# Ten expert weight blocks loaded ahead of the routed experts in place of eight, and the first four experts written out ahead of the loop

## The chip, the cores and the metric

One Trainium2 chip, one core. The metric is the device time of one launch in microseconds (us); the kernel before takes 1544.34 us, the median of three runs from 1542.98 to 1544.42.

## What is computed

Two transformer blocks over 256 tokens of width 1024, all in f32. The first block is a token mixer (sliding window attention beside a gated spatial unit), a layer norm, a layer of 32 routed experts (each token goes to 4) and a second layer norm. The second block (a recurrent mixer beside a block attention, then a convolutional FFN) follows; the change does not touch it.

```python
def expert_block(args):                       # per expert e, its tokens xb
    gt = jnp.minimum(xb @ w_gate[e] + b_gate[e], SWIGLU_LIMIT)
    up = jnp.clip(xb @ w_up[e] + b_up[e], -SWIGLU_LIMIT, SWIGLU_LIMIT)
    hid = gt * jax.nn.sigmoid(SWIGLU_ALPHA * gt) * (up + 1.0)
    return hid @ w_down[e] + b_down[e]
# first block: x = LN1(ALPHA1*x + mixer(x));  x = LN2(ALPHA1*x + sum over 4 experts of gate*expert(x))
```

Each expert has three 1024x1024 f32 matrices, 12 MB; all 32 are read once, 403 MB.

## The kernel before

**Blocks and slots.** The host lays an expert's weights out as 6 blocks of 2 MB, 4096 floats in each of 128 partitions: 4 "up" blocks (gate and up matrices) and 2 "down" blocks. There are 192 blocks, numbered here as loads 0 to 191 in the order of use. They go through a ring of `RING` = 8 slots in SBUF: slots 0 to 5 are the tensor `ring`, slots 6 and 7 are pieces of the tensor `work`. Load n lies in slot n % 8.

**Who waits for whom.** TensorE (PE) counts the semaphore `slots_used` up by one after the matmuls of each block (L746 for up, L776 for down). SyncE (SP) issues all weight loads on one queue, in program order. Load n from 8 on is issued in `refill` once `slots_used` is at least n - 7, so when the block that lies 8 before it has been used:

```python
sp.wait_ge(slots_used, sp.snap(it * (TURN * SLOTS) + (load - RING + 1)))
sp.dma_start(slot_area(s), expert_slot(e, load % SLOTS)).then_inc(slot_in[s], 16)
```

PE waits for `slot_in[s]` before a block's first matmul (L738, L769).

**The stage before the experts.** SP first issues the token mixer's inputs and weights. The last two are `x` (L470) and five broadcast rows of 1024 floats (`rows`, L471: `b_out`, `ln1_g`, `ln1_b`, `ln2_g`, `ln2_b`). VectorE (DVE) waits for these two before L1608. SP then waits for the end of attention (`attn_done`) to issue the expert biases (L474), and then loads 0 to 7 as the mixer's weights, whose room the slots share, fall free: 0, 1, 2, 3 and 6 after the projections, 4 and 5 behind two steps of the output projection, 7 last (L476 to L493), behind five small loads for the second block.

**The experts.** PE, ScalarE (ACT), DVE and SP each run a loop over 8 iterations of `TURN` = 4 experts (L778, L1305, L1753, L505), with counts from the router's result. In an expert PE does 4 up blocks (L743), gathers the next expert's tokens (L695), transposes, does 2 down blocks (L774) and scatters the result (L707) in the next one.

**Behind the experts.** SP issues the first weight halves of the second block into ring slots 0 and 1: `lora` (two halves of 0.75 MB) and `r` (L521), once `slots_used` says that slots 0 to 3 are free. GpSimd (POOL) casts the first lora half (L2118), DVE subtracts (L1770, called by `rest_half("lora", (0,))` at L1772), and only then does DVE, in its program order, start the second layer norm (L1630, from L1776). ACT casts the second lora half (L1314), then loads its table and does the norm's square root (L1329).

Of the kernel before, what the change touches and what calls it, by code (L numbers as in the profile page):

```python
# [16 lines left out]
P = 128  # L17
T = 256
TT = T // P
D = 1024  # L20
KD = D // P
# [8 lines left out]
PASSES = T // CAP  # L30
COLS = NE * PASSES + 2
# [4 lines left out]
RING = 8  # L36
TURN = 4
PER_TURN = TURN * SLOTS // RING
SPLITS = 3
# [76 lines left out]
def program(nc, A, out):  # L116
    ctx = ExitStack()
    with ctx:
# [11 lines left out]
        work, work_parts = area("work", 27500)  # L130
# [3 lines left out]
        def take(floats):  # L134
            a = work[:, top[0]:top[0] + floats]
            top[0] += floats
            assert top[0] <= 27500, top
            return a
# [36 lines left out]
        n_iter = ctx.enter_context(nc.sbuf_tensor("n_iter", [1, 2], I32))  # L175

# [27 lines left out]
        chosen4 = sq.rearrange("p t c -> p (t c)")[:, 0:TT * TOPK * NE].rearrange("p (t k e) -> p t k e", t=TT, k=TOPK)  # L204
# [4 lines left out]
        hid, yy = pool2[:, 0:512], pool2[:, 512:1024]  # L209
        hidT = pool2[:, 1024:1536].rearrange("p (j c) -> p j c", j=4)  # L210
# [10 lines left out]
        consts_in, w_g_in, w_u_in = sem("consts_in"), sem("w_g_in"), sem("w_u_in")  # L221
        ln_rows_in, wsT_in = sem("ln_rows_in"), sem("wsT_in")
# [217 lines left out]
        def slot_of(turn, j):  # L440

            return (turn * SLOTS + j) % RING

        def landed_count(it, turn, j):

            return (it * PER_TURN + (turn * SLOTS + j) // RING + 1) * 16

        def up_slot(s):

            return slot_area(s).rearrange("p (b k n) -> p b k n", b=2, k=2)  # L450

        def down_slot(s):
            return slot_area(s).rearrange("p (k n) -> p k n", k=4)

        @block.sync
        def _(sp):
# [8 lines left out]
            sp.dma_start(w_in[:, :, W_QKV + G1:], A["w_in"][:, :, W_QKV + G1:]).then_inc(w_g_in, 16)  # L465
# [4 lines left out]
            sp.dma_start(x_nat, A["x"].rearrange("(t p) d -> p t d", p=P)).then_inc(ln_rows_in, 16)  # L470
            sp.dma_start(rows_sb[:, 0:mix_at], A["rows"][0:mix_at].partition_broadcast(P)).then_inc(ln_rows_in, 16)  # L471
# [4 lines left out]
            for s in (0, 1, 2, 3, 6, 4, 5, 7):  # L476
# [5 lines left out]
                if s == 5:  # L482
                    sp.wait_ge(mix_done, 4)
# [9 lines left out]
                sp.dma_start(slot_area(s), expert_slot(s // SLOTS, s % SLOTS)).then_inc(slot_in[s], 16)  # L493
# [4 lines left out]
            def refill(it, load):  # L498

                s = load % RING  # L500
# [56 lines left out]
        def _(pe):  # L557
# [41 lines left out]
            pe.wait_ge(w_g_in, 16)  # L599
# [128 lines left out]
            def expert(it, turn):  # L728

                now, ahead = pe.snap(it * TURN + (turn + 1)), pe.snap(it * TURN + (turn + 2))  # L730
# [5 lines left out]
                for j in range(UP_SLOTS):  # L736
                    s = slot_of(turn, j)
                    pe.wait_ge(slot_in[s], pe.snap(landed_count(it, turn, j)))  # L738
                    w = up_slot(s)
                    for kk in range(2):  # L740
                        for b, to in enumerate((gate_bank, up_bank)):
                            for n2 in range(2):
                                ins = pe.matmul(to[n2 * CAP:(n2 + 1) * CAP, :], x_e[:, 2 * j + kk, :],  # L743
                                                w[:, b, kk, n2 * BANK:(n2 + 1) * BANK],
                                                start=False, stop=j == UP_SLOTS - 1 and kk == 1)
# [21 lines left out]
                for j in range(SLOTS - UP_SLOTS):  # L767
                    s = slot_of(turn, UP_SLOTS + j)
                    pe.wait_ge(slot_in[s], pe.snap(landed_count(it, turn, UP_SLOTS + j)))  # L769
                    w = down_slot(s)  # L770
                    for kk in range(4):
                        k = 4 * j + kk
                        for n2 in range(2):
                            ins = pe.matmul(y_bank[n2 * CAP:(n2 + 1) * CAP, :], hidT[:, k % 4, k // 4 * CAP:(k // 4 + 1) * CAP],  # L774
                                            w[:, kk, n2 * BANK:(n2 + 1) * BANK], start=False, stop=k == KD - 1)
                    ins.then_inc(slots_used, 1)  # L776

            with pe.Fori(0, n) as it:  # L778
# [438 lines left out]
        def _(act):  # L1217
# [75 lines left out]
            def expert(it, turn):  # L1293

                now, ahead = act.snap(it * TURN + (turn + 1)), act.snap(it * TURN + (turn + 2))
# [6 lines left out]
                act.wait_ge(slots_used, act.snap(it * (TURN * SLOTS) + (turn + 1) * SLOTS))  # L1302
                act.copy(yy, bank[7][:, :]).then_inc(y_ready, 1)  # L1303

            with act.Fori(0, n) as it:  # L1305
# [218 lines left out]
        def _(dve):  # L1524
# [82 lines left out]
            dve.wait_ge(ln_rows_in, 32)  # L1607
# [127 lines left out]
            def expert(it, turn):  # L1735

                now = dve.snap(it * TURN + (turn + 1))
                dve.wait_ge(slots_used, dve.snap(it * (TURN * SLOTS) + (turn * SLOTS + UP_SLOTS)))
# [14 lines left out]
            with dve.Fori(0, n) as it:  # L1753
# [19 lines left out]

            for t in range(TT):
# [428 lines left out]
```

## Time and profile before

| | |
|---|---|
| median of 3 runs | 1544.34 us |
| profiled execution | 1542.65 us, span 1540.5 us |
| granted TensorE clock, mean | 0.994 |
| PE / DVE / ACT / POOL busy | 93% / 33% / 21% / 4% of the span |
| stages | mixer to 117 us, experts 117 to 1031 us, second block to the end |
| chain of work that ended last | PE 58%, DMA 34%, DVE 5%, ACT 2% of the span |

The profiled execution takes 2.15 us more than its span. The chain of work is followed back from the last instruction, at each step to what released it. Times in the rows are from the start of the span.

### The profile page before, as it was taken

The page shows a single profiled execution, that of the slowest core. Times are in us where ns is not written, and L with a number is a line of the kernel's source. Part 1 is how long each engine was busy: PE and PEld are TensorE (multiplying, and loading weights), DVE is VectorE, ACT ScalarE, POOL GpSimd, SP SyncE. Part 2 cuts the span into 40 slices and gives each one's busy share as a digit, 9 for nine tenths or more (in the row PEclk, how much of TensorE's full clock was granted, in tenths as well). Part 3 has the DMA queues.
Part 4 walks back from the last instruction along what each step waited for, and adds up shares of the span by engine and source line. Part 5 has one row for each costly group of instructions (what it writes and reads, how often), then busy time and mean ns, then how long its engine had stood idle before and what let it go on. Part 6 is the DMA issues. An engine that isn't in the chain of part 4 may idle for free.

```text
span 1540.5 us, 21839 instructions
## 1 busy us (share of the span) xinstructions
PE 1437.0 (93%) x9246; PEld 783.7 (51%) x9246; DVE 512.3 (33%) x880; ACT 329.8 (21%) x480; POOL 64.8 (4%) x32
## 2 busy tenths in 40 slices
PE   8989999999989989989998998978999999999998
PEld 6543333333333333333333333328878895499997
DVE  1762211112112112112111111137797455365665
ACT  0531110001001001001000000015555220244442
POOL 0000000000000000000000000000000000022231
PEclk9999999999999999999999999998999999999999
DMA  9589999999999999999999999983441106145552
GB/s 363 225 343 403 428 427 428 429 428 429 429 429 428 428 429 429 429 428 429 428 429 428 428 429 429 428 355 110 164 164 55 56 2 246 41 157 198 177 191 82
DMA packets 44533, 491.33 MB, mean 319 GB/s; under 512 B 4944, under 2 KB 5456, under 8 KB 13168
## 3 DMA queue, kind: packets, MB, share of 16 engines
q1 hardware_dynamic: 44352, 490.66, 77.4%
q8 instruction: 28, 0.46, 0.1%
q10 hardware_dynamic: 144, 0.13, 0.0%
q14 instruction: 9, 0.07, 0.0%
HBM read 489.73 MB, written 1.05 MB: 319 GB/s over the span
## 4 chain that ended last, share of the span: by engine, by line
PE 58%; DMA 34%; DVE 5%; ACT 2%; issue 1%; SPq 0%; DVEq 0%; ACTq 0%
DMA ring<-in_w_exp 27%; PE bank L743 12%; PE bank L774 8%; DMA work<-in_w_exp 7%; PE bank L800 6%; PE bank L801 6%; PE bank L802 6%; PE bank L707 2%; PE bank L1137 2%; PE bank L644 2%; PE bank L1175 2%; PE bank L695 2%; PE bank L565 1%; PE bank L595 1%; PE bank L715 1%; ACT work L1301 1%
## 5 line engine op out<-in xcount | busy, mean ns | idle before, releaser
L743 PE MATMUL bank<-ring,work 128*64 128x512 f32 x1536 | 346.3, 596 | 31.1 <-DMA ring<-in_w_exp 31.0
L1739 DVE TENSOR_SCALAR work<-bank 128x512 f32<-128x512 f32 x32 | 22.1, 692 | 748.0 <-PE bank L743 748.0
L743 PEld LDWEIGHTS bank<-ring,work 128*64 128x64 f32 x1536 | 105.5, 136 | 256.4 <-issue 178.6
L774 PE MATMUL bank<-ring,work 128*64 128x512 f32 x768 | 170.1, 595 | 16.8 <-ACT work L1301 16.8
L800 PE MATMUL bank<-work_parts,ring_parts 128*128 128x256 f32 x472 | 132.8, 281 | 4.5 <-DVE work_parts L1794 4.5
L1297 ACT ACTIVATE work<-work 128x512 f32<-128x512 f32 x32 | 20.2, 630 | 538.6 <-DVE work L1739 538.6
L801 PE MATMUL bank<-work_parts,ring_parts 128*128 128x256 f32 x472 | 133.4, 283 | 0.0
L802 PE MATMUL bank<-work_parts,ring_parts 128*128 128x256 f32 x472 | 133.3, 282 | 0.0
L743 PE MATMUL bank<-work 128*64 128x512 f32 x512 | 115.5, 595 | 11.3 <-DMA work<-in_w_exp 11.3
L774 PEld LDWEIGHTS bank<-ring,work 128*64 128x64 f32 x768 | 53.7, 137 | 117.8 <-issue 103.2
L800 PEld LDWEIGHTS bank<-work_parts,ring_parts 128*128 128x128 f32 x472 | 91.3, 193 | 5.6 <-issue 4.8
L801 PEld LDWEIGHTS bank<-work_parts,ring_parts 128*128 128x128 f32 x472 | 90.6, 192 | 0.8
L802 PEld LDWEIGHTS bank<-work_parts,ring_parts 128*128 128x128 f32 x472 | 90.9, 192 | 0.0
L800 PE MATMUL bank<-ring_parts,work_parts 128*128 128x512 f32 x200 | 79.7, 398 | 3.1 <-DVE ring_parts L1770 2.4
L743 PEld LDWEIGHTS bank<-work 128*64 128x64 f32 x512 | 34.8, 135 | 86.8 <-issue 59.5
L801 PE MATMUL bank<-ring_parts,work_parts 128*128 128x512 f32 x200 | 78.7, 394 | 0.0
L802 PE MATMUL bank<-ring_parts,work_parts 128*128 128x512 f32 x200 | 78.6, 393 | 0.0
L707 PE MATMUL bank<-work 64*128 64x512 f32 x264 | 74.3, 641 | 0.7 <-ACT work L1303 0.7
L1477 ACT CAST ring_parts<-ring 128x2048 fp32r<-128x2048 f32 (+1 forms) x44 | 63.4, 1467 | 50.3 <-PE bank L802 50.3
L1303 ACT COPY work<-bank 128x512 f32<-128x512 f32 x32 | 18.8, 587 | 230.6 <-PE bank L774 230.6
L2130 POOL TENSOR_TENSOR ring_parts<-ring,ring_parts 128x1024 fp32r<-128x1024 f32 x22 | 55.9, 2539 | 224.0 <-ACT ring_parts L1477 224.0
L695 PEld LDWEIGHTS bank<-work 128*128 128x128 bf16 x1584 | 49.1, 97 | 27.5 <-issue 26.9
(390 smaller groups left out, 1638.7 us busy)
## 6 DMA issues: line engine op xcount, KB each, us to landing
ring<-in_w_exp SPq DMA_DIRECT2D x144, 2048.0 KB, 33.6
work<-in_w_exp SPq DMA_DIRECT2D x48, 2048.0 KB, 33.6
ring<-in_ffn_up SPq DMA_DIRECT2D x22, 1024.0 KB, 4.8
ring<-in_ffn_down SPq DMA_DIRECT2D x22, 512.0 KB, 3.3
ring<-in_w_in SPq DMA_DIRECT2D x2, 2048.0 KB, 17.6
ring<-in_w_out SPq DMA_DIRECT2D x4, 1024.0 KB, 17.4
ring<-in_w_k SPq DMA_DIRECT2D x4, 1024.0 KB, 5.0
ring<-in_w_v SPq DMA_DIRECT2D x4, 1024.0 KB, 4.9
```

What stands on the lines that cost most here:

```text
L644: ins = pe.matmul(bank[mix_bank[t][n]][:, :], mixT[:, k, t * P:(t + 1) * P], w_out[:, k, n * BANK:(n + 1) * BANK], start=k == 0, stop=k == ...
L695: ins = pe.matmul(x_bank[:, k * CAP:(k + 1) * CAP], h_part[:, part, t, k * P:(k + 1) * P], place[:, t, :], start=k == 0 and (t, part) == P ...
L707: ins = pe.matmul(bank[2 * t + n][:, :], place_T[lo:lo + CAP, t * P:(t + 1) * P], yy[lo:lo + CAP, :], start=False, stop=stop, skip_group_c ...
L743: ins = pe.matmul(to[n2 * CAP:(n2 + 1) * CAP, :], x_e[:, 2 * j + kk, :], w[:, b, kk, n2 * BANK:(n2 + 1) * BANK], start=False, stop=j == UP ...
L774: ins = pe.matmul(y_bank[n2 * CAP:(n2 + 1) * CAP, :], hidT[:, k % 4, k // 4 * CAP:(k // 4 + 1) * CAP], w[:, kk, n2 * BANK:(n2 + 1) * BANK] ...
L800: pe.matmul(to, left[0], right[0], start=start, stop=False, skip_group_check=True)
L801: pe.matmul(to, left[0], right[1], start=False, stop=False, skip_group_check=True)
L802: return pe.matmul(to, left[1], right[0], start=False, stop=stop, skip_group_check=True)
L1137: ins = pe.matmul(bank[to[n2] + t][:, :], yT[:, k, t * P:(t + 1) * P], tail[f][:, k, n2 * BANK:(n2 + 1) * BANK], start=k == 0, stop=k == N ...
L1175: ins = pe.matmul(bank[2 * t + n2][:, :], mT[:, k, t * P:(t + 1) * P], tail["out0" if k < 4 else "out1"][:, k % 4, n2 * BANK:(n2 + 1) * BANK],
L1477: act.copy(ff_hi[i][:, cols], ff_land[i][:, cols]).then_inc(ff_upper[i], 1)
L2130: pool.tensor_tensor(ff_rest[i][:, 2 * D:FF], ff_land[i][:, 2 * D:FF], ff_hi[i][:, 2 * D:FF].bitcast(F32), ALU.subtract).then_inc(down_res ...
```

## The change

Three things are changed together.

1. **Two more blocks before the loop.** Loads 7 and 8 get room of their own, outside the ring. Loads 0 to 6 go to slots 0 to 6, load 7 (`NINTH`) lies in a new tensor `spare`, load 8 (`TENTH`) in four quarters: one in `spare`, two in the place of the rows `ln2_g` and `ln2_b`, one in `sq`, a scratch of the token mixer; load 9 (`FIRST - 1`) goes to slot 7. The new room comes from the DMA scratch, which is set to 256 bytes per partition. Load 7 and three quarters of load 8 are issued right behind the late rows, ahead of the wait for attention; the last quarter once `sgu_ready` says that `sq` is free.
2. **Late rows.** The load of rows ahead of the loop shrinks from 5 to 3 rows; the two rows of the second layer norm are loaded behind the last refill, and DVE waits for them before that norm.
3. **Refills.** The two rooms are used once. Load n from 17 on is issued, as before, once n - 7 blocks are used (it lies in slot (n - 2) % 8); loads 10 to 16 once 1 to 7 are. The first four experts are written out ahead of the loop on PE, ACT, DVE and SP with waits against constants, and the loop runs 7 times. The wait ahead of the lora halves goes from 20 used blocks of the last 24 to 22.

```diff
+FIRST = 10
+NINTH, TENTH = 7, 8
+DMA_SCRATCH = 256
+        spare, _ = area("spare", SLOT + D)
+        ninth, tenth_first = spare[:, 0:SLOT], spare[:, SLOT:]
+        tenth = [tenth_first, rows_sb[:, ln2_at:ln2_at + D], rows_sb[:, ln2_at + D:ln2_at + 2 * D], sq.rearrange("p t c -> p (t c)")]
...
-        def slot_of(turn, j):
-            return (turn * SLOTS + j) % RING
+        def slot_of(load):
+            return (load - (FIRST - RING)) % RING if load >= FIRST else min(load, RING - 1)
...
-            sp.dma_start(rows_sb[:, 0:mix_at], A["rows"][0:mix_at].partition_broadcast(P)).then_inc(ln_rows_in, 16)
+            sp.dma_start(rows_sb[:, 0:ln2_at], A["rows"][0:ln2_at].partition_broadcast(P)).then_inc(late_in, 16)
+            sp.dma_start(ninth, expert_slot(NINTH // SLOTS, NINTH % SLOTS)).then_inc(late_in, 16)
+            for n in range(3):
+                sp.dma_start(tenth[n], tenth_part(n)).then_inc(late_in, 16)
...
                 if s == 5:
+                    sp.wait_ge(sgu_ready, 1)
+                    sp.dma_start(tenth[3], tenth_part(3)).then_inc(w_g_sq_in, 16)
                     sp.wait_ge(mix_done, 4)
...
-                sp.dma_start(slot_area(s), expert_slot(s // SLOTS, s % SLOTS)).then_inc(slot_in[s], 16)
+                load = s if s < RING - 1 else FIRST - 1
+                sp.dma_start(slot_area(s), expert_slot(load // SLOTS, load % SLOTS)).then_inc(slot_in[s], 16)
+            def first_refill(load):
+                sp.wait_ge(slots_used, load - FIRST + 1 if load < FIRST + RING - 1 else load - RING + 1)
+                s = slot_of(load)
+                sp.dma_start(slot_area(s), expert_slot(load // SLOTS, load % SLOTS)).then_inc(slot_in[s], 16)
...
-            with sp.Fori(0, n_rest) as it:
-                for load in range(RING, RING + TURN * SLOTS):
+            for load in range(FIRST, FIRST + TURN * SLOTS):
+                first_refill(load)
+            with sp.Fori(1, n_rest) as it:
+                for load in range(FIRST, FIRST + TURN * SLOTS):
                     refill(it, load)
-            for load in range(RING, TURN * SLOTS):
+            for load in range(FIRST, TURN * SLOTS):
                 refill(n_rest, load)
+            sp.dma_start(rows_sb[:, ln2_at:ln2_at + 2 * D], A["rows"][ln2_at:ln2_at + 2 * D].partition_broadcast(P)).then_inc(late_in, 16)
...
-                    sp.wait_ge(slots_used, sp.snap(n_rest * (TURN * SLOTS) + (TURN * SLOTS - RING + 4)))
+                    sp.wait_ge(slots_used, sp.snap(n_rest * (TURN * SLOTS) + (TURN * SLOTS - 2)))
...
-            with pe.Fori(0, n) as it:
+            for turn in range(TURN):
+                expert(0, turn)
+            with pe.Fori(1, n) as it:
                 for turn in range(TURN):
                     expert(it, turn)
...
-            dve.wait_ge(ln_rows_in, 32)
+            dve.wait_ge(late_in, 6 * 16)
...
             rest_half("lora", (0,))
+            dve.wait_ge(late_in, 7 * 16)
...
-    nc = bacc.Bacc("TRN2", target_bir_lowering=False, num_devices=1)
+    nc = bacc.Bacc("TRN2", target_bir_lowering=False, num_devices=1, dynamic_dma_scratch_size=DMA_SCRATCH)
```

**SP's queue ahead of the experts.** `in_w_exp` are the expert blocks, `in_rows` the broadcast rows, `in_bias` the expert biases. Before:

```order
L470 DMA work<-in_x 128x2x1024
L471 DMA work<-in_rows 128x5120
L474 DMA work<-in_bias 96x3072 [waits attn_done]
L493 DMA ring<-in_w_exp 128x4096 [waits proj_done]
L493 DMA ring<-in_w_exp 128x4096 x3
L493 DMA work<-in_w_exp 128x4096 [waits ug_biased,mixed_done]
L493 DMA ring<-in_w_exp 128x4096 [waits mix_first]
L493 DMA ring<-in_w_exp 128x4096 [waits mix_done]
```

Now:

```order
L475 DMA work<-in_x 128x2x1024
L476 DMA work<-in_rows 128x3072
L477 DMA spare<-in_w_exp 128x4096
L483 DMA spare<-in_w_exp 128x1024
L483 DMA work<-in_w_exp 128x1024 x2
L486 DMA work<-in_bias 96x3072 [waits attn_done]
L508 DMA ring<-in_w_exp 128x4096 [waits proj_done]
L508 DMA ring<-in_w_exp 128x4096 x3
L508 DMA work<-in_w_exp 128x4096 [waits ug_biased,mixed_done]
L508 DMA ring<-in_w_exp 128x4096 [waits mix_first]
L496 DMA work<-in_w_exp 128x1024 [waits sgu_ready]
L508 DMA ring<-in_w_exp 128x4096 [waits mix_done]
```

One block and three quarters stand ahead of the biases, and the last quarter ahead of the load that waits for `mix_done`.

**SP's queue behind the last refill.** Before, the last refills and what follows (`in_w_lora` and `in_w_r` are the second block's first weights):

```order
L502 REGISTER_ALU
L503 ISA [waits slots_used]
L503 DMA work<-in_w_exp 128x4096
L517 REGISTER_ALU
L521 DMA ring<-in_w_lora 128x1536 [waits slots_used]
L521 DMA ring<-in_w_lora 128x1536
L521 DMA ring<-in_w_r 128x2048 x2
```

Now:

```order
L523 REGISTER_ALU
L524 ISA [waits slots_used]
L524 DMA ring<-in_w_exp 128x4096
L533 DMA work<-in_rows 128x2048
L541 REGISTER_ALU
L545 DMA ring<-in_w_lora 128x1536 [waits slots_used]
L545 DMA ring<-in_w_lora 128x1536
L545 DMA ring<-in_w_r 128x2048 x2
```

The two late rows, 1 MB, stand between the last expert block and the lora halves.

## Rows read from the trace of the kernel before

**Rows 1.** The page's 40 slices: share of DMA time, and GB/s.
```profile
DMA  9589999999999999999999999983441106145552
GB/s 363 225 343 403 428 427 428 429 428 429 429 429 428 428 429 429 429 428 429 428 429 428 428 429 429 428 355 110 164 164 55 56 2 246 41 157 198 177 191 82
```

**Rows 2.** Chain that ended last: start us, us, what; experts 0, 9, 31.
```profile
117.25 6.87 PE bank L743 x32
...
359.36 6.90 PE bank L743 x32
...
366.45 33.05 DMA work<-in_w_exp
...
980.88 35.27 DMA ring<-in_w_exp
```

**Rows 3.** Issues of expert blocks from 99 to 116 us, with times to landing.
```profile
L493 SPq DMA_DIRECT2D ring<-in_w_exp x1: 328/328/328, 100.1 to 100.1; - x1
L493 SPq DMA_DIRECT2D work<-in_w_exp x1: 328/328/328, 115.5 to 115.5; - x1
DMA to landing us min/median/max: 7.5/7.8/8.0
```

**Rows 4.** The same for load 8, the first refill.
```profile
L503 SPq DMA_DIRECT2D ring<-in_w_exp x1: 351/351/351, 121.0 to 121.0; - x1
DMA to landing us min/median/max: 9.0/9.0/9.0
```

**Rows 5.** The same for loads 17 and 18.
```profile
L503 SPq DMA_DIRECT2D ring<-in_w_exp x2: 332/334/336, 159.3 to 167.4; - x2
DMA to landing us min/median/max: 11.9/13.5/15.1
```

**Rows 6.** The same for load 19.
```profile
L503 SPq DMA_DIRECT2D ring<-in_w_exp x1: 333/333/333, 170.8 to 170.8; - x1
DMA to landing us min/median/max: 13.4/13.4/13.4
```

**Rows 7.** The same for load 191, the last block.
```profile
L503 SPq DMA_DIRECT2D work<-in_w_exp x1: 332/332/332, 990.7 to 990.7; - x1
DMA to landing us min/median/max: 35.3/35.3/35.3
```

**Rows 8.** Windows by stage: PE, PEld, DVE, ACT, POOL busy, clock, DMA share, GB/s.
```profile
50.00:55.00 5.00, 4.44 (x17) 2.56 (x18) 3.77 (x5) 4.54 (x8) 0.00 (x0) 1.00 0.02 9
55.00:60.00 5.00, 5.00 (x37) 2.81 (x37) 3.15 (x5) 2.94 (x4) 0.00 (x0) 1.00 0.00 0
```

**Rows 9.** DMA issues by tensor: KB each, us to landing; SP's timeline.
```profile
work<-in_rows SPq DMA_DIRECT2D x1, 2560.0 KB, 24.5
...
27.27 1.28 SPq L471 DMA_DIRECT2D work<-in_rows  x1
...
61.31 0.34 SPq L474 DMA_DIRECT2D work<-in_bias  x1
```

**Rows 10.** DVE's timeline at the instruction that waits for the late loads.
```profile
68.98 2.28 DVE L1608 SCALAR_TENSOR_TENSOR work<-work 128x2048 f32<-128x2048 f32 x1
```

**Rows 11.** Timelines of POOL, DVE and ACT behind the experts.
```profile
1027.88 1.46 POOL L2118 CAST ring_parts<-ring 128x1536 fp32r<-128x1536 f32 x1 [925.75 <-DMA ring<-in_w_lora]
...
1029.38 1.76 DVE L1770 TENSOR_TENSOR ring_parts<-ring,ring_parts 128x1536 fp32r<-128x1536 f32 x1 [4.67 <-POOL ring_parts L2118]
1033.22 1.43 DVE L1630 BATCH_NORM_STATS2 work<-bank 128x6 f32<-128x512 f32 x2 [2.08 <-PE bank L707]
...
1031.88 1.48 ACT L1314 CAST ring_parts<-ring 128x1536 fp32r<-128x1536 f32 x1
1033.38 1.28 ACT L1329 ACT_TABLE_LOAD   x1
```

**Rows 12.** DMA queues of the page: packets, MB, share of 16 engines.
```profile
q1 hardware_dynamic: 44352, 490.66, 77.4%
q8 instruction: 28, 0.46, 0.1%
```

More of the change, by code:

```diff
@@ L30 @@
 PASSES = T // CAP
+WORK = 27500
 COLS = NE * PASSES + 2
@@ L129, in program @@
         ring, ring_parts = area("ring", SLOTS * SLOT)
-        work, work_parts = area("work", 27500)
+        work, work_parts = area("work", WORK)
         bank = [ctx.enter_context(nc.psum_tensor(f"bank{i}", [P, BANK], F32)) for i in range(8)]
@@ L136, in take @@
             top[0] += floats
-            assert top[0] <= 27500, top
+            assert top[0] <= WORK, top
             return a
@@ L438, in slot_area, with landed_count @@
             return ring[:, s * SLOT:(s + 1) * SLOT] if s < SLOTS else work[:, (seventh_at, eighth_at)[s - SLOTS]:][:, 0:SLOT]
-        def slot_of(turn, j):
-            return (turn * SLOTS + j) % RING
-        def landed_count(it, turn, j):
-            return (it * PER_TURN + (turn * SLOTS + j) // RING + 1) * 16
+        def slot_of(load):
+            return (load - (FIRST - RING)) % RING if load >= FIRST else min(load, RING - 1)
+        def landed_count(it, load):
+            return (it * PER_TURN + (load - (FIRST - RING)) // RING + 1) * 16
         def up_slot(s):
-            return slot_area(s).rearrange("p (b k n) -> p b k n", b=2, k=2)
-        def down_slot(s):
-            return slot_area(s).rearrange("p (k n) -> p k n", k=4)
+            return [slot_area(s)[:, n * D:(n + 1) * D] for n in range(4)]
         @block.sync
@@ L498, in refill @@
             def refill(it, load):
-                s = load % RING
+                s = slot_of(load)
                 e = (it * TURN + load // SLOTS) % NE
@@ L728, in expert, with landed @@
             def expert(it, turn):
-                now, ahead = pe.snap(it * TURN + (turn + 1)), pe.snap(it * TURN + (turn + 2))
+                in_loop = not isinstance(it, int)
+                value = pe.snap if in_loop else int
+                now, ahead = value(it * TURN + (turn + 1)), value(it * TURN + (turn + 2))
+                def landed(load):
+                    if not in_loop and load in (NINTH, TENTH):
+                        pe.wait_ge(late_in, 6 * 16)
+                        if load == TENTH:
+                            pe.wait_ge(w_g_sq_in, 2 * 16)
+                        return [ninth[:, n * D:(n + 1) * D] for n in range(4)] if load == NINTH else tenth
+                    s = slot_of(load + TURN * SLOTS if in_loop else load)
+                    pe.wait_ge(slot_in[s], value(landed_count(it, load)) if in_loop or load >= FIRST else 16)
+                    return up_slot(s)
                 pe.wait_ge(place_T_ready, now)
@@ L736, in expert @@
                 for j in range(UP_SLOTS):
[L737 to L739 removed]
+                    w = landed(turn * SLOTS + j)
                     for kk in range(2):
@@ L1293, in expert @@
             def expert(it, turn):
-                now, ahead = act.snap(it * TURN + (turn + 1)), act.snap(it * TURN + (turn + 2))
+                value = int if isinstance(it, int) else act.snap
+                now, ahead = value(it * TURN + (turn + 1)), value(it * TURN + (turn + 2))
                 act.wait_ge(gt_ready, now)
@@ L1301, in expert @@
                 act.copy(hidT, bank[4][:, :].rearrange("p (j c) -> p j c", j=4)).then_inc(hidT_ready, 1)
-                act.wait_ge(slots_used, act.snap(it * (TURN * SLOTS) + (turn + 1) * SLOTS))
+                act.wait_ge(slots_used, value(it * (TURN * SLOTS) + (turn + 1) * SLOTS))
                 act.copy(yy, bank[7][:, :]).then_inc(y_ready, 1)
-            with act.Fori(0, n) as it:
+            for turn in range(TURN):
+                expert(0, turn)
+            with act.Fori(1, n) as it:
                 for turn in range(TURN):
@@ L1751, in expert @@
                 build_place_g(it * TURN + (turn + 1))
-            with dve.Fori(0, n) as it:
+            for turn in range(TURN):
+                expert(0, turn)
+            with dve.Fori(1, n) as it:
                 for turn in range(TURN):
```

28 lines of the change are left out of this document (15 added, 13 removed).

## The prediction

> **What bounds the kernel now.** I read the page's slices first. The DMA row stands at 9 and the rate at 427 to 429 GB/s from slice 5 to slice 25, so through nearly all of the expert stage [rows 1]. A saturated DMA does not yet say that DMA sets the end, so the chain of waits comes next. It runs through PE from the first expert at 117.25 us to the tenth at 359.36 us [rows 2], nine experts in 242.1 us, 26.90 us each or 4.48 us per block. From 366.45 us on the long pieces are DMA (one of 33.05 us there, one of 35.27 us at 980.88 us) [rows 2]: PE has caught up with the loads and stays behind them to the end of the stage. The pace of the loads comes from two landings. Load 18 is issued at 167.4 us and lands 11.9 us later, at 179.3 us [rows 5]. The last block, load 191, is issued at 990.7 us and lands 35.3 us later, at 1026.0 us [rows 7]. That is 173 blocks in 846.7 us, 4.894 us each, 29.4 us per expert. So PE gains 2.5 us per expert on the loads until it has eaten its lead, and the stage ends a fixed piece of work behind the last landings. **The end moves by what the stream of loads moves, and PE's early lead is worth nothing by itself.** What counts is at which time load n lands, for n above about 20.
>
> **Room ahead of the loop.** Behind the late rows, issued at 27.27 us and landed 24.5 us later at 51.8 us, the queue stands empty until the biases are issued at 61.31 us [rows 9]: the windows from 50 to 60 us show 9 and 0 GB/s [rows 8]. The change adds 1.75 blocks there and takes 1 MB of rows, half a block, out. 1.25 blocks at 4.894 us are 6.1 us, so the late loads land near 58 us. That is 3 us ahead of the biases and 11 us ahead of DVE's L1608, which waits for them and ran at 68.98 us [rows 10]. Cost of this part: nothing, and if that cover were gone the first expert would start later one for one. The last quarter of load 8 is 1.2 us of DMA, ahead of load 5, which is issued at 100.1 us and lands at 107.6 us [rows 3]; it is the last block of the first expert, which starts at 117.25 us [rows 2], so the cover is over 10 us. Nothing again.
>
> **Refills.** Two blocks more at the start should be worth 2 x 4.894 = 9.8 us of DMA time at the end. This holds only if the queue never runs empty in between, and here it does. The two rooms are used once. Loads 10 to 16 take the places in the queue that loads 8 to 14 had, so load 16 lands when load 14 did: load 17 landed at 159.3 + 15.1 = 174.4 us [rows 5], three blocks earlier is 159.7 us. Load 17, though, must wait as before for ten used blocks, and load 18 for eleven. PE's pace sets these times, and PE runs no faster: 159.3 and 167.4 us, when both were issued before [rows 5]. A transfer that meets an empty queue takes 7.5 to 8.0 us from issue to landing [rows 3], not 4.9. So:
>
> - Load 17: issued at 159.3 us, when load 16 has 0.4 us to its landing and nothing is queued; lands at 166.8 to 167.3 us.
> - Load 18: issued at 167.4 us, on an empty queue again; lands at 174.9 to 175.4 us. Before: 179.3 us. **Gain 3.9 to 4.4 us, I take 4.1.**
> - Load 19: issued at 170.8 us [rows 6], 4 us ahead of that landing, so it follows one block time behind. The nearest row for a second transfer behind a lone one is load 8: load 7 was issued at 115.5 us and landed at 123.5 us [rows 3], load 8 was issued at 121.0 us and landed at 130.0 us [rows 4], 6.5 us later and not 4.9. It was issued only 2.5 us ahead of the landing, load 19 will be 4 us ahead; I take 4.9, and keep 1.6 us less gain as the bound.
> - Load 24, the next tight one, comes an expert after load 18, at 194.3 us; load 23 lands near 200 us. From here PE's pace of 4.48 us against 4.894 us widens the lead, and the queue is never empty again.
>
> The stream thus keeps 4.1 of its 9.8 us; 5.7 us are lost in two gaps, near 158 to 160 us and 166 to 168 us. From below: 2.3 us. From above: a restart with no cost of its own would land load 18 at 167.4 + 4.9 = 172.3 us, a gain of 7.0 us.
>
> A rule on the lone transfer: the Trainium skill (DMA: Bandwidth & Descriptors, Anatomy of one DMA) fits 2.0 us plus the bytes over 436 GB/s, 6.8 us for 2 MB, which would land load 18 at 174.2 us and make the gain 5.1 us. The page measured another issuing path; the rows here say 7.5 to 8.0 us, and I go by them.
>
> **Peeled experts.** Four experts' instructions are written once more on four engines, and register arithmetic and one branch go. PE waits for nothing of either between experts in this chain, and the peeled experts lie in the stretch in which PE has a lead, so I take nothing for both.
>
> **Behind the experts.** The two late rows are half a block, 2.45 us, between the last block and the lora halves. The first half landed at 1027.88 us, where POOL starts; DVE's subtraction at 1029.38 us took 1.76 us, and DVE then stood idle 2.08 us before its norm at 1033.22 us [rows 11]. Relative to the experts' end, POOL now starts at 1030.33 us, the subtraction at 1031.83 us, and it ends at 1033.59 us: the norm starts **0.4 us later**, on the path that sets the end. ACT's cast at 1031.88 us [rows 11] waits for the second half, now near 1032.3 us; cast and table load end near 1035.1 us, just ahead of the statistics that the next instruction needs. The wait for 22 used blocks in place of 20 costs nothing, since two expert blocks and the rows are still queued when it passes. Bounds of this part: 0 and 1.6 us (the lone-start excess above, if the rows' load should break the stream).
>
> **The sum.** -4.1 + 0.4 = -3.7 us: 1542.65 us of the profiled execution become 1538.9 us. That execution is 1.7 us below the median of the runs; against the median of 1544.34 us I forecast 1540.6 us, 0.24% less. A measurement here can tell about 0.2%, 3.1 us, from no change, so this forecast lies just over that line.
>
> **Rivals.**
>
> - *A, the full two blocks.* If the queue did not run empty at loads 17 and 18, -9.8 + 0.4 us: 1534.9 us. For it: the expert stage is bound by DMA all through the page's slices [rows 1]. Against it: the issue times of rows 5 and PE's pace in rows 2. It would need PE 8 us ahead of itself by the second expert. Chance 0.07.
> - *B, given back on the way.* Restart at its worse bound (2.3 us), or the experts' written-out code fetched beside full DMA engines. The page counts 28 instruction packets, 16 KB each [rows 12]; four more experts are about five packets (an estimate, by PE's share of executed instructions). At 4.894 us for eight rows of 16 KB per engine, a packet delays its engine by 0.6 us if it is not shared out: up to 3.1 us. Result -0.5 to -2 us, 1543.1 us in the middle: within 0.2%. Against the code's share: the loads keep 4.9 us per block at 159 to 180 us, where PE goes through its loop for the first time. Chance 0.25. The Trainium skill (Runtime: NRT & Kernel Launch, Instruction fetch mechanics) says that crossing a fetch block is mostly hidden, while a taken branch out of the window stalls; the first would take the 3.1 us away.
> - *C, slower.* The DMA scratch falls to 256 bytes. Should the queue lose depth by it, every refill pays: before, seven blocks are in flight (35.3 us at 4.894 us [rows 7]). The stream has 174 blocks behind load 17; at 0.04 us more per block the whole gain and 3.1 us on top are gone, and at 1% more (0.05 us) the result is +4.8 us, 1549.1 us; one block in flight at 7.5 us each would be over 400 us. For it: nothing in the profile shows what the scratch serves. Against it: all weights go through a queue of the kind hardware_dynamic [rows 12]. Chance 0.06. The Trainium skill (SBUF — State Buffer, size table) calls this scratch the ring of the software path, which SP's loads do not use; by it C would not occur.
>
> **How the numbers follow.** The forecast has 0.62, with its own range of -2.3 to -5.5 us (1538.8 to 1542.0 us); of that 0.12 falls short of 3.1 us. Faster by over 0.2%: 0.50 + 0.07 = 0.57. Within: 0.12 + 0.25 = 0.37. Slower: 0.06. The range goes from 1538.0 us, the forecast's good end with the runs' spread of 0.1%, to 1544.3 us, B's poor end and no change at all; A and C stay out.
>
> **What would show it.** Right: load 17 issued near 159 us and load 18 near 167 us, both landing 7.5 to 8 us later, with a dip in the DMA windows there; then 4.89 us per block; the last block landing near 1022 us instead of 1026.0; DVE's idle time before the norm gone. PE should still take 26.9 us per expert at first, and be caught by the loads about 1.7 experts later than at 366 us (4.1 us over 2.5 us per expert). Wrong: a load 17 that lands before 165 us (A), a pace above 4.90 us per block (C, or B's code), or a first expert that starts later than 117.25 us.

## The result, and the profile after

The changed kernel takes 1546.47 us, the median of 19 runs (1543.57 to 1555.64); the kernel before takes 1543.69 us beside it (19 runs, 1541.99 to 1546.18). The ratio is 1.0026, 95% interval 1.0014 to 1.0039: **slower by 0.26%**, where 0.24% faster was forecast. (The ratios here and below are over all the runs, the long ones included, and the times are medians; the medians are 2.8 us or 0.18% apart.) The profiled execution takes 1546.09 us (span 1544.3 us, granted clock 0.991), 3.8 us of span more than before's. The runs do not spread evenly: 13 of the 19 lie between 1543.6 and 1547.9 us, four between 1551.4 and 1552.2, the last two at 1554.4 and 1555.6; before's reach no further than 1546.2.

**The expert stage did nearly what was forecast.** The page of the changed kernel, its clock, its slices and its queues:

```profile
PEclk9999999999999999999999999989999989999999
DMA  9789899999999999999999999974442005145552
GB/s 364 291 355 405 357 427 426 428 428 428 429 429 428 428 428 428 428 429 429 429 429 428 428 428 429 428 328 137 148 153 101 10 1 245 41 154 200 177 190 81
...
q1 hardware_dynamic: 44928, 490.66, 77.5%
q8 instruction: 33, 0.54, 0.1%
```

The rate is as before, 426 to 429 GB/s from the sixth slice on [rows 1], the bytes are the same, and five more packets of instructions moved, as estimated [rows 12]. The windows of the changed kernel (columns as in [rows 8]):

```profile
50.00:55.00 5.00, 4.25 (x16) 2.46 (x17) 3.77 (x6) 4.34 (x8) 0.00 (x0) 1.00 0.99 397
55.00:60.00 5.00, 5.00 (x35) 2.72 (x35) 3.15 (x5) 3.05 (x4) 0.00 (x0) 1.00 0.13 48
158.00:168.00 10.00, 9.33 (x88) 4.29 (x86) 4.03 (x10) 1.80 (x3) 0.00 (x0) 1.00 0.58 211
```

and of the kernel before, for the third of them:

```profile
158.00:168.00 10.00, 9.32 (x88) 4.33 (x86) 4.03 (x10) 1.80 (x3) 0.00 (x0) 1.00 1.00 424
```

The early loads fill what was an empty queue from 50 us and are done near 56 us. The dip stands where it was forecast: from 158 to 168 us DMA is busy 0.58 of the time. The issues of loads 17, 18 and 19 in the changed kernel, KB and us as in [rows 5, 6]:

```profile
L514 SPq DMA_DIRECT2D work<-in_w_exp x1: 328/328/328, 159.1 to 159.1; - x1
L514 SPq DMA_DIRECT2D ring<-in_w_exp x1: 328/328/328, 167.2 to 167.2; - x1
DMA to landing us min/median/max: 7.7/7.7/7.8
...
L514 SPq DMA_DIRECT2D ring<-in_w_exp x1: 328/328/328, 170.6 to 170.6; - x1
DMA to landing us min/median/max: 10.2/10.2/10.2
```

Load 17 lands at 166.8 us, load 18 at 167.2 + 7.8 = 175.0 us against 179.3 before: 4.3 us gained, 4.1 were taken. Load 19 lands at 180.8 us, 5.8 us behind load 18 where I took 4.9: before, it landed at 170.8 + 13.4 = 184.2 us [rows 6], so 3.4 us of the gain are left. The chain of waits of the changed kernel, start and us:

```profile
117.25 6.87 PE bank L778 x32
...
405.59 7.12 PE bank L807 x32
412.86 32.85 DMA work<-in_w_exp
...
978.41 35.29 DMA ring<-in_w_exp
...
1017.44 10.44 DMA ring<-in_w_lora
1027.93 1.47 POOL ring_parts L2160
1029.43 1.36 DVE ring_parts L1811
...
1034.57 1.28 DVE work L1679
...
1216.80 2.00 PE bank L1065 x16
...
1263.37 2.00 PE bank L1065 x16
```

PE is caught by the loads at 412.86 us and not at 366.45 [rows 2], 46.4 us or 1.7 experts later. The last long piece ends at 978.41 + 35.29 = 1013.70 us against 1016.15 [rows 2]: **2.45 us ahead**. DVE's timeline of the changed kernel behind the experts:

```profile
1029.43 1.76 DVE L1811 TENSOR_TENSOR ring_parts<-ring,ring_parts 128x1536 fp32r<-128x1536 f32 x1 [7.17 <-POOL ring_parts L2160]
1031.10 1.42 DVE L1668 BATCH_NORM_STATS2 work<-bank 128x6 f32<-128x512 f32 x2
```

The norm has no idle time ahead of it any more and starts at 1031.10 us, 2.12 us ahead of before's 1033.22 [rows 11]. The 2.45 us have become 2.12, so 0.33 us are lost behind the experts, where the late rows were put.

**The loss lies elsewhere.** The chain rows at 1216.80 and 1263.37 us are the same two places of the second block as these in the chain of the kernel before:

```profile
1219.37 2.00 PE bank L1030 x16
...
1258.44 2.00 PE bank L1030 x16
```

At the first the change is 2.57 us ahead, at the second 4.93 us behind: 7.5 us are lost in 46 us, in code that the change does not touch. PE's waits in the changed kernel (us in total, times, longest):

```profile
PE bank L778 <- DMA ring<-in_w_exp: 30.8, 47, 1.3
...
PE bank L1115 <- issue: 1.7, 1, 1.7
...
PE bank L1111 <- issue: 0.5, 1, 0.5
```

"Issue" is a wait for nothing that the profile shows. L1111 to L1119 are small matmuls of the recurrence in two bursts; the first is 352 instructions (176 matmuls, each with its weight load), the second 288. Before, the first took 2.4 us, and neither had such a wait. PE's timeline at the place, in the changed kernel:

```profile
1229.94 0.27 PE L1115 MATMUL bank<-ring,work 32*64 32x64 f32 x1 [1.70 <-issue]
1229.95 0.38 PE L1119 MATMUL bank<-work 32*64 32x64 f32 x8
```

These nine matmuls are the last of the burst. The windows around it, of the changed kernel:

```profile
1220.00:1230.00 10.00, 8.10 (x226) 7.43 (x226) 2.69 (x5) 2.07 (x4) 0.00 (x0) 1.00 0.01 2
1230.00:1240.00 10.00, 10.00 (x107) 9.00 (x107) 4.38 (x11) 0.00 (x0) 0.00 (x0) 0.61 0.01 2
1240.00:1250.00 10.00, 9.97 (x93) 8.55 (x94) 5.42 (x13) 0.89 (x3) 1.27 (x1) 0.71 0.01 2
```

and of the kernel before:

```profile
1220.00:1230.00 10.00, 9.81 (x198) 9.06 (x200) 4.16 (x8) 2.35 (x4) 0.00 (x0) 1.00 0.01 3
1230.00:1240.00 10.00, 10.00 (x217) 9.12 (x209) 4.71 (x12) 0.65 (x2) 0.00 (x0) 1.00 0.01 3
1240.00:1250.00 10.00, 9.46 (x80) 8.22 (x77) 7.52 (x16) 2.15 (x4) 2.54 (x2) 1.00 0.00 1
```

Before, PE is busy 9.81 us of the first window and keeps the full clock. In the changed kernel it pauses, and right behind the pause the granted clock falls from 2.4 to 1.2 GHz for a stretch, which makes 0.61 and 0.71 of the next two windows: (0.39 + 0.29) x 10 = 6.8 us of clock at most, since PE is not bound by it throughout. The other part is the pause, 1.9 us between two matmuls of the burst. Behind the second place the pause of the second burst adds 0.5 us, and 1.6 us come back by the end: before has a short stretch at the low clock near 1348 us, in its execution, that the changed one lacks.

### The profile page after: what moved, and what is told of

Its sections match the earlier page's. It is cut to its first block, busy times and chain, and to the rows that moved or that the text cites. A ratio compares the mean times of both kernels' runs of the same rounds, so it can differ in the third digit from the quotient of the medians.

```text
span 1544.3 us, 21709 instructions
## 1 busy us (share of the span) xinstructions
PE 1440.8 (93%) x9246; PEld 786.9 (51%) x9246; DVE 512.3 (33%) x880; ACT 320.9 (21%) x473; POOL 64.7 (4%) x32
## 4 chain that ended last, share of the span: by engine, by line
PE 60%; DMA 32%; DVE 5%; ACT 2%; issue 1%; POOL 0%; SPq 0%; DVEq 0%; ACTq 0%
DMA ring<-in_w_exp 22%; PE bank L778 13%; DMA work<-in_w_exp 9%; PE bank L807 8%; PE bank L835 6%; PE bank L836 6%; PE bank L837 6%; PE bank L731 2%; PE bank L1172 2%; PE bank L668 2%; PE bank L1210 2%; PE bank L719 2%; PE bank L589 1%; PE bank L619 1%; PE bank L739 1%; DMA ring<-in_w_lora 1%
## 5 line engine op out<-in xcount | busy, mean ns | idle before, releaser
L778 PE MATMUL bank<-work 128*64 128x512 f32 x492 | 110.9, 595 | 9.9 <-DMA work<-in_w_exp 9.9
```

## The experiments

**Theory and rivals.** The peeled experts are 1325 more PE instructions. The traces show most of them: an f32 matmul of the kernel is two matmul and two weight load records, a bf16 matmul or an f32 transpose one of each, so four experts are 656 and 656. The other 13 are waits and register work, counted in the compiled programs, which no trace shows. All later code stands 1325 further on. A packet of instructions is 16 KB (0.46 MB in 28 [rows 12]), 256 instructions of 64 bytes. The theory: code is fetched in blocks of 256 instructions, a burst of hundreds of small instructions is eaten faster than the next block comes, and whether a block's edge falls where it hurts depends on the code's position modulo 256, which the peel moved. The Trainium skill (Runtime: NRT & Kernel Launch, Instruction fetch mechanics) gives the same blocks and calls crossing one "mostly hidden". Rivals: the loss comes from the loads' change (late rows, new room); from the amount of code; or from where PE stands in time when it gets there. The probe is a pad of small matmuls behind the experts' last scatter, where PE waits for the norm, into a bank that is written over before it is read. A pad is named by its instructions. The expectations of the first four runs count the peel as 1373 instructions, an f32 transpose as four; it is 1325.

### 1. The change, with 164 instructions of padding

```diff
+            for _ in range(82):
+                pe.matmul(bank[5][0:32, 0:32], sel[0:32, 0:32], bias_parts[0:32, 0:32], start=True, stop=True, skip_group_check=True)
             def transpose_hn(...
```

> The change with 82 tiny bf16 matmuls (32x32, two instructions each, 164 in all) on TensorE behind the last scatter, where TensorE waits some 8 us for the norm; they write a bank that is overwritten later. They move all of TensorE's later code by 164 instructions, so that with the 1373 that the change adds it stands 1537 = 6 x 256 + 1 behind where it stood before. Theory F (TensorE's instruction fetch in the recurrence's bursts of small matmuls comes late because the code has moved against the blocks of 256 instructions, and the pause also brings the clock down): the gaps of 1.9 and 0.7 us are gone, no stretch of 13.65 us at clock 0.5 near 1230 us, the span 2 to 3.5 us shorter than before (1537 to 1539 us). Theory T (the clock falls because the burst now comes 2.5 us earlier in time): the gaps and the low stretch stay, about 4 us slower than before.

Measured: 1540.59 us (11 runs, 1538.37 to 1542.68) against 1544.46: ratio 0.9975, 0.9967 to 0.9984. More code made the change **faster** by 5.9 us in the medians. The windows of this kernel keep the clock:

```profile
1220.00:1230.00 10.00, 9.81 (x245) 9.13 (x244) 3.81 (x8) 2.35 (x4) 0.00 (x0) 1.00 0.01 3
1230.00:1240.00 10.00, 10.00 (x161) 9.07 (x161) 5.63 (x15) 0.65 (x2) 0.00 (x0) 1.00 0.02 3
```

No wait "issue" stands at the bursts. The loads' part, the late rows and the peel are all still in, so none of them costs what was lost. The gain against before is 3.9 us, the forecast's 3.7. The expectation named the right outcome for a wrong position: it took the code to stand 1 instruction over a multiple of 256 from before's, and it stands 209 over. That 209 has no pause either was luck.

This run also answers the rival of the time of arrival. It reaches the first chain place at 1217.86 us, before at 1219.37, run 6 at 1218.45 and run 3 at 1221.55 us, all without a pause. The changed kernel and runs 2, 4, 5 and 7, with pauses, arrive at 1216.80 to 1223.24 us, so both kinds arrive at the same times.

### 2, 3. The kernel before, with 92 and with 256 instructions of padding

The same lines with `range(46)` and `range(128)`, and nothing of the change.

> The kernel before with 46 such matmuls (92 instructions) at the same place: the alignment of the changed kernel (1373 is 93 over a multiple of 256), and nothing else of the change. Theory F: gaps of about 1.9 and 0.7 us in the two bursts, the low clock stretch in most executions, 4 to 10 us slower than before (1548 to 1554 us). Theory T, and any theory that puts the loss on the loads, the rows or the scratch: within 1 us of before.

> The kernel before with 128 such matmuls, 256 instructions: the alignment of before. Control for the padding itself. Theory F: no gap, within 1 us of before. If padding costs time by itself, or its activity shifts the clock: slower by that, as much as or more than in the run with 92.

Measured: 92 instructions give 1543.37 us (ratio 0.9999, 0.9991 to 1.0008). A pause has come, PE's waits of this kernel,

```profile
PE bank L1083 <- issue: 0.9, 1, 0.9
```

but the clock stays at 1.00 behind it. A whole block of 256 gives 1544.76 us (1.0001, 0.9993 to 1.001) and, as before, no pause. So position makes pauses, in code that is otherwise the same. The 4 to 10 us that were expected of run 2 did not come; its position, 92, is not the changed kernel's 45. Between the two chain places of the section above run 2 takes 40.22 us, before 39.07 (1258.44 - 1219.37): the pause costs its own length there, too little to show in the medians.

### 4. The peel alone

```diff
...
-            with pe.Fori(0, n) as it:
+            for turn in range(TURN):
+                expert(0, turn)
+            with pe.Fori(1, n) as it:
...
```

On PE only, without the loads' change.

> The kernel before with only TensorE's first four experts written out ahead of its loop (eight blocks ahead, loads, rows, scratch and the other engines as before): adds 1372 instructions, one fewer than the change. Theory F: gaps and clock stretch as in the changed kernel, and without its gain of 2.5 us in the loads 4 to 10 us slower than before. A theory that puts the loss on the loads or rows: within 1 us of before.

Measured: 1544.24 us (12 runs) against 1544.46: ratio 1.0017, 0.9997 to 1.0037, which alone settles nothing and is not the 4 to 10 us expected, but the 12 runs tell more: seven at 1542.0 to 1544.3 us (clock 0.995 to 0.997), three at 1548.9 to 1549.5 (0.991 to 0.992), one at 1555.2 (0.987), one at 1558.3 (0.984). The steps of 0.004 in the clock are 6.2 us of 1545. The profiled execution, 1548.87 us, shows the waits "issue" at the bursts, 2.2 us in two, and no low clock behind them: between the two chain places it takes 40.70 us, 1.6 more than before. The rest of its lateness is older: the granted clock is 0.53 from 110 to 120 us, its first expert starts at 119.78 us and its last long piece ends 3.9 us later than before's. So a long time of this kernel need not come from a low stretch at the burst.

### 5. The kernel before, with 44 instructions: the peel's position without the peel

The same lines with `range(22)`. 1325 and 1324 are 45 and 44 modulo 256.

> The kernel before with 22 tiny matmuls (44 instructions) behind the last scatter. The pauses of the first four runs show that TensorE's f32 transposes are two instructions and not four: the change adds 1325 instructions (45 over a multiple of 256) and the peel alone 1324 (44), so the 164 of the first run gave another alignment than before, and the 92 of the second another than the change. This run has the alignment of the peel, with nothing else of the change. Theory F (late instruction fetch, then low clock): a pause of 1.7 to 1.9 us behind some 335 instructions of the first burst and one of 0.7 to 1.0 us behind some 264 of the second; single executions spread from about 1543 to above 1550 us; median 2 to 6 us above before. A theory that needs the peel, the loads or the rows: within 1 us of before, spread of 5 us at most.

Measured: 1545.48 us (12 runs) against 1544.23: ratio 1.0029, 1.001 to 1.0048. Nine runs lie at 1544.3 to 1547.7 us, one at 1551.4, two at 1558.2. By the ratios, twenty-two idle matmuls cost about what the change does; in the medians it is 1.3 us, below the 2 to 6 expected. The amount of code and the loads are out as a cause; the position is shown. This profiled execution (1544.33 us) has the pause and keeps the clock.

### 6, 7. The peel with 164 instructions; the change with 256

> TensorE's peel alone with the 164 instructions of padding that took the pauses out of the change. Theory F: no pauses, no spread, within 1 us of before: the peel costs nothing where its code stands well, and the whole gain of the padded change is the loads'. If the peel costs or gains by itself: another time than before with no pause.

> The change with 256 instructions of padding: its own alignment kept. Control that the 164 cured by alignment and not by being there. Theory F: pauses of about 1.9 and 0.7 us as in the change, median 1 to 6 us above before, executions above 1550 us among them. If padding cures by itself: as the run with 164, 3 to 4 us faster than before.

Measured: peel and 164, 1544.26 us (1.0005, 0.9996 to 1.0014), no pause and no run above 1546.9. The change and a whole block, 1547.08 us (1.003, 1.0013 to 1.0046), with the pauses back (waits of 1.1 and 0.7 us at the bursts, the first shorter than the 1.9 expected) and four of 12 runs at 1552.5 to 1554.6. Together, by position, with the longest time between two matmuls of the first burst, all of the profiled executions:

| code moved by, modulo 256 | kernels | pause, us | between the two chain places, us | runs far above the rest |
|---|---|---|---|---|
| 0 | before; 3 | none | 39.07; 39.14 | none |
| 208, 209 | 6; 1 | none | 39.07; 39.07 | none |
| 92 | 2 | 1.08 | 40.22 | none |
| 44 | 4; 5 | 1.65; 1.64 | 40.70; 40.70 | 5 of 12; 3 of 12 |
| 45 | 7 | 1.34 | 40.43 | 4 of 12 |
| 45 | the change | 1.92 | 46.57 | 6 of 19 |

The pause comes and goes with the position, whether peel and loads are there or not; its length at one position is not fixed (1.34 and 1.92 us at 45). In each row the pause costs its length; the changed kernel's execution lost another 5.6 us, with the clock.

Where the pause stands tells more. In the four kernels at 44 and 45 exactly 9 matmuls, 18 instructions, of the first burst come behind it; in run 2, at 92, it is 33 matmuls, 66 instructions. The code moved 47 or 48 instructions further, and the pause came 48 instructions earlier: it stands at a fixed place of the code's count and not of the burst, as an edge between blocks would. By the same count an edge lies inside the burst of runs 1 and 6 too, some 182 instructions ahead of its end and 170 behind its start, and makes no pause there; at position 0 it lies past the burst's end. So an edge in a burst is not enough; behind 286 and 334 instructions of the burst it made one, behind 170 none. That the next block is asked for about one block ahead, and that this is what the burst outruns, would fit all rows but was not measured.

### 8. A pause of 1 us made by hand

The kernel before, its code where it was. In the middle of each burst PE hands a semaphore to POOL, which does five copies (two, for the second burst) and hands it back.

```diff
+                        if (b, m) == (1, 3):
+                            ins.then_inc(mix_first, 1)
+                            pe.wait_ge(bias_less, 3 + tt)
...
+                pool.wait_ge(mix_first, 2 + tt)
+                for n in range((5, 2)[tt]):
+                    at = 16 * (n + 5 * tt)
+                    ins = pool.tensor_copy(alpha_ident[:, at:at + 16], ident[:, at:at + 16])
+                ins.then_inc(bias_less, 1)
```

> The kernel before, with its own code alignment, and a pause made by hand: ahead of the last quarter's matmuls in each of the two bursts TensorE waits for GpSimd, which does five small copies (16 columns each) in the first and two in the second; some 1 to 2 us and 0.5 to 1 us. Theory F in full (it is TensorE's pause inside the burst, whatever makes it, that lets the clock fall): no wait for instructions, single executions spread up to 1550 us or more as in the runs with pauses, median 1.5 to 4 us above before. If the low clock needs late instruction fetch or moved code: slower by the two pauses alone, 1 to 3 us, with no execution more than 3 us above the median.

Measured: pauses of 1.07 and 0.68 us; 1543.67 us (1.0003, 0.9994 to 1.0012), no low stretch, 40.16 us between the chain places. This agrees with run 2, and leaves open whether a longer one would do it.

### 9. A pause of 1.9 us made by hand

The same with `(12, 3)` copies of 8 columns.

> As the run before, with twelve small copies in the first burst and three in the second, so that the pauses are as long as those of late instruction fetch (the run before made 1.07 and 0.68 us; now some 2.0 and 0.8 us), the code where it stood before. Theory F in full (the length of TensorE's pause decides, whatever makes it): executions above 1549 us among them at a clock of 0.990 or less, median 2 to 5 us above before. If the low clock needs late instruction fetch: 1 to 2.5 us slower, no execution more than 3 us above the median.

Measured: 1546.09 us (12 runs) against 1544.76: ratio 1.0018, 1.0007 to 1.0029; eight runs at 1544.5 to 1547.9, four at 1551.0 to 1552.2. The profiled execution is one of the four. Its POOL timeline, PE's wait, the windows and the two chain rows:

```profile
1232.68 1.56 POOL L2132 COPY work<-work 128x8 f32<-128x8 f32 x12 [22.91 <-PE bank L1087]
```

```profile
PE bank L1079 <- POOL work L2132: 2.3, 2, 1.7
```

```profile
1220.00:1230.00 10.00, 9.81 (x89) 9.23 (x89) 4.05 (x7) 3.15 (x6) 0.00 (x0) 1.00 0.01 2
1230.00:1240.00 10.00, 8.32 (x237) 7.71 (x235) 4.99 (x13) 0.00 (x0) 1.56 (x12) 0.84 0.01 3
1240.00:1250.00 10.00, 10.00 (x102) 8.67 (x100) 1.35 (x4) 0.65 (x2) 0.00 (x0) 0.50 0.01 2
```

```profile
1221.38 2.00 PE bank L1030 x16
...
1267.87 2.00 PE bank L1030 x16
```

The pause is 1.89 us between matmuls, as in the changed kernel, and the low clock follows it here too, without any instruction moved in front of it: 46.49 us between the chain rows, for 46.57 in the changed kernel and 39.07 before. So the low clock needs neither the moved code nor a late fetch; a pause made by other means will do, though in the medians it costs 1.3 us and not the 2 to 5 expected, and eight of the 12 runs show no long time.

### 10. Both new rooms used twice

The padded change of run 1, with a second use of the two rooms. Loads 17 and 18 go where 7 and 8 were, once those are used, so that load 17 waits for 8 used blocks in place of 10 and the stream stays two blocks deeper through load 26; the ring's slots are renumbered for that, the wait ahead of the lora halves goes back to 20 used blocks, and the late rows go behind both lora halves.

```diff
...
-                sp.wait_ge(slots_used, load - FIRST + 1 if load < FIRST + RING - 1 else load - RING + 1)
+                sp.wait_ge(slots_used, load - FIRST + 1 if load < 27 else load - RING + 1)
+                if load == 17:
+                    sp.dma_start(ninth, expert_slot(load // SLOTS, load % SLOTS)).then_inc(w_out_in, 16)
+                    return
+                if load == 18:
+                    for n in range(4):
+                        sp.dma_start(tenth[n], tenth_part(n, load)).then_inc(wsT_in, 16)
+                    return
...
```

> The padded change (164) with the two extra rooms used a second time, for loads 17 and 18, so that loads 17 to 26 are issued 9 blocks behind the last used one and only those from 27 on 7 behind; the ring's slots are renamed so that the last four blocks lie away from the room of the next weights, and the late rows are loaded behind both lora halves. Theory: the queue no longer runs empty at loads 17 and 18, only load 30 is tight (issued 2 us ahead of the landing in front of it, 1 to 1.6 us lost): the last blocks land 7 to 9 us earlier than before, 1536 to 1539 us. If the early gaps are not what limits the gain: as the padded change, 1540.6 us.

Measured: 1535.98 us (6 runs, 1532.34 to 1537.55) against 1544.23: ratio 0.9947, 0.9935 to 0.996, **faster by 8.3 us**, and the fastest kernel here. Of this kernel the window at the old dip, then the issues of loads 27 and 28:

```profile
158.00:168.00 10.00, 9.32 (x88) 4.31 (x86) 4.04 (x10) 1.80 (x3) 0.00 (x0) 1.00 0.99 406
```

```profile
L523 SPq DMA_DIRECT2D ring<-in_w_exp x2: 327/328/328, 207.8 to 212.5; - x2
DMA to landing us min/median/max: 9.1/9.4/9.6
```

and its chain and DVE's timeline behind the experts:

```profile
976.39 35.29 DMA ring<-in_w_exp
```

```profile
1028.81 1.43 DVE L1683 BATCH_NORM_STATS2 work<-bank 128x6 f32<-128x512 f32 x2 [2.15 <-PE bank L740]
```

The dip is gone, 0.99 for 0.58. The long piece ends at 1011.68 us, 4.5 us ahead of before, although PE began its experts 3.0 us later in this execution (120.21 us for 117.25), so that the refills that wait for it were late as well. Loads 27 and 28 land 9.1 to 9.6 us after issue, near the 7.5 to 8.0 us of an empty queue: here the lead is thin, where load 30 was expected to be the tight one. DVE is idle before the norm again, as in [rows 11], so the rows cost nothing where they now stand. How much of the step from run 1, 4.6 us in the medians, is the rooms, how much the rows and how much the earlier wait ahead of the lora halves was not separated.

## Why the prediction was wrong

**The step that failed** is "Peeled experts": PE "waits for nothing of either between experts in this chain, and the peeled experts lie in the stretch in which PE has a lead, so I take nothing for both". True of the experts: PE's pace and lead were as before. Not asked was what 1325 instructions do to the code behind them. They put pauses of 1.9 and 0.7 us into two bursts of the second block, and the first brought the low clock behind it in the profiled execution. That turns −3.9 us (run 1) into +2.8 us. Runs 1, 5 and 7, and the place of the pause in run 2, show the position; run 9 shows that a pause alone can bring the clock down.

**Rival B** had the right suspect, the fetch of written-out code, and the wrong place: it priced packets that delay loads. The five packets came, and the pace of the loads did not change: load 191 is in flight for 35.3 us as before. The Trainium skill (Runtime: NRT & Kernel Launch, Instruction fetch mechanics) calls crossing a block "mostly hidden". Outside the two bursts the trace agrees, as far as PE's waits tell: no wait "issue" is there that before lacks. Inside them it does not, with waits of 1.7 and 0.5 us.

Point by point for the rest:

- *What bounds, and where the gain must be looked for:* right. PE's early lead moved from 366 to 413 us and the end followed the loads.
- *Room ahead of the loop, at no cost:* right; done near 56 us where 58 was taken, first expert at 117.25 us in both.
- *Refills, 4.1 us:* load 18 gained 4.3, but the last block only 2.45. About 0.9 us went at load 19, 5.8 us behind load 18 (the bound of 1.6 was the right row to keep, the value of 4.9 too hopeful). A further 0.6 us was gone by load 28, near 225 us, and 0.35 us over the 163 blocks that follow.
- *Behind the experts, +0.4 us:* measured 0.33.
- *The sum without the step that failed:* −3.7 forecast, −3.9 in run 1. That they agree so closely is in part luck. In the profiled pair the two terms come to −2.45 + 0.33 = −2.1 us and not −3.7, and the time outside the span is some 0.3 us shorter (1.8 for 2.15), for which the sum had no term. In another pair, runs 1 and 3, whose first experts start at 118.97 and 119.54 us, the last long pieces end 3.8 us apart. So the gain differs by execution, and what makes up the 3.9 us of the medians was not found.
- *A, two full blocks:* refuted as argued, load 17 landed at 166.8 us and not before 165. Run 10 shows what it lacked, a second use of the rooms.
- *C, the scratch:* no block in flight was lost, 35.29 us for 35.27.

The range ended at 1544.3 us because every case was a case of the loads. None held that moved code could cost something in a stage that the change leaves alone. (The forecast's own good end, −5.5 us, is not worked out from its bounds, whose best case is a gain of 7.0 us; it did not matter here.)

**Open.** The profiled execution of the changed kernel has the low stretch and still is one of the 13 lower runs, so that stretch by itself does not put an execution among the six far above. Low stretches come elsewhere too: every profiled execution has them near 1040 us and at the end, and eight of the twelve have one near 110 us as well, with the first expert at 118.97 to 120.74 us in place of 116.79 to 117.26. Open are also why the low clock follows the pause in some executions only, and how many of the times far above the rest are of that kind: one execution of each kernel was profiled, and at positions 44 and 45 three of four keep the clock behind pauses of 1.34 to 1.65 us, one of them in an execution that is long for another reason (run 4). That long times come with the position is shown: 18 of 55 runs at 44 and 45, none at the others without a pause made by hand. That each of them has the low stretch at the burst is not.

## What to carry to other kernels

Where a change adds or removes hundreds of instructions on an engine, look for its dense bursts of small instructions everywhere behind that point: compare the waits put down to "issue" before and after, and try the change with a few padding widths before it is judged. A gain of a quarter of a per cent can be hidden, or made up, by where the code happens to lie. And room that lets loads run ahead once is worth only the queue time that it fills; ask at once whether it can be used a second time, when the queue would next run empty.

## What was not expected of the hardware

- Waits that the profile puts down to nothing reached 1.7 us inside a dense burst of small matmuls. One packet of instructions (the view does not say for which engine) moves in the changed kernel's window from 1226 to 1231 us, the 13th of 40 slices of its DMA row, so at 1227.5 us:

```profile
GB/s 0 0 0 0 0 0 0 0 0 0 0 0 131 0 0 0 0 0 0 0 0 0 0 0 0 0 0 0 0 0 0 0 0 0 0 0 0 0 0 0
q8 instruction: 1, 0.02, 1.1%
```

  The next matmul of the burst starts at 1229.94 us, 2.4 us later. In the kernel before, one moves at 1229.9 us, 0.8 us before the burst's end, and nothing waits. That it is the packet that PE waited for is not shown; that the pause stands at a place fixed by the code's count is (experiments, after runs 6 and 7).
- A pause of about 1.9 us in an otherwise busy PE was followed by a granted clock of 1.2 GHz for some 14 us in two profiled executions (1232 us in the changed kernel, 1236.8 us in run 9), 5.5 to 5.6 us on top of the pause; pauses of 1.07 to 1.65 us were not, in five others. These seven executions draw no line between the two.
